# Layer normalisation of a decoder trunk: the last weight panel chunk by chunk with the first sums inside it, one activation table for logarithm and exponential, five mean subtractions on GpSimd, rounded products first

## The reference, cut to what matters

```python
x = layer_norm(DEEPNORM_ALPHA * x + f(x), g, b)

def layer_norm(x, g, b):
    mu = jnp.mean(xf, -1, keepdims=True)
    var = jnp.mean(jnp.square(xf - mu), -1, keepdims=True)
    return (xf - mu) * lax.rsqrt(var + LN_EPS) * g + b
```

## Time and profile before

| what | us |
|---|---|
| median of three runs | 1171.61 |
| the runs | 1167.24 to 1173.54 |
| span of the profiled execution | 1171.3 |
| TensorE busy | 1092.9 (93%) |
| VectorE busy | 704.1 (60%) |
| ScalarE busy | 543.7 (46%) |
| GpSimd busy | 300.1 (26%) |

### The profile page before, as it was taken

One profiled execution on the slowest core, in us unless ns is written; L12 is line 12 of the kernel. 1 busy time (PEld: TensorE's weight loads), 2 busy tenths in 40 slices (PEclk: granted clock), 3 DMA queues, 4 the chain that ended last, 5 costly groups with the idle time before them and its releaser, 6 DMA issues.

```text
span 1171.3 us, 20048 instructions
## 1 busy us (share of the span) xinstructions
PE 1092.9 (93%) x6991; PEld 986.4 (84%) x6991; DVE 704.1 (60%) x1203; ACT 543.7 (46%) x860; POOL 300.1 (26%) x285
## 2 busy tenths in 40 slices
PE   6999979978999998897999999989999799999997
PEld 5999869666666665496999999979999799999996
DVE  4843643677777777548666663365564866665344
ACT  4337511256666666536444443343343544444324
POOL 8400123302677777134000000123003400000111
PEclk9989969988999999898999999989999899999998
DMA  7424200267998996542444443534445244444321
GB/s 228 158 101 149 73 1 1 98 223 259 304 305 307 303 308 219 177 150 72 143 143 143 143 148 130 175 96 143 144 144 153 72 143 147 159 156 157 127 87 46
DMA packets 120882, 182.59 MB, mean 156 GB/s; under 512 B 6224, under 2 KB 61615, under 8 KB 120750
## 3 DMA queue, kind: packets, MB, share of 16 engines
q1 hardware_dynamic: 118402, 174.61, 44.8%
q0 software_dynamic: 2416, 7.16, 2.1%
HBM read 176.12 MB, written 5.63 MB: 155 GB/s over the span
## 4 chain that ended last, share of the span: by engine, by line
PE 80%; DVE 12%; issue 4%; ACT 3%; DMA 1%; POOL 0%; DVEq 0%; SPq 0%; ACTq 0%; POOLq 0%
PE bank L1736 74%; PE bank L2051 4%; DVE kTl L1157 2%; DVE lo L1150 1%; DMA raw<-w_in_mix 1%; ACT hi L751 1%; DVE xres L1583 1%; DVE xres L1157 1%; DVE sbias L1458 1%; PE bank L2253 1%; DVE gs L1454 1%; DVE sbias L1449 1%; PE bank L2184 0%; DVE work L1157 0%; DVE xl L1590 0%
## 5 line engine op out<-in xcount | busy, mean ns | idle before, releaser
L1736 PE MATMUL bank<-xh,hi 128*128 128x320 f32 x1184 | 373.9, 316 | 24.4 <-DVE xl L1590 18.4
L1736 PE MATMUL bank<-xl,hi 128*128 128x320 f32 x1184 | 371.1, 313 | 0.0
L1736 PE MATMUL bank<-xh,lo 128*128 128x320 f32 x1184 | 370.9, 313 | 0.0
L1150 DVE TENSOR_TENSOR lo<-raw,hi 128x2048 fp32r<-128x2048 f32 x102 | 240.4, 2357 | 188.5 <-ACT hi L751 188.5
L751 ACT ACTIVATE hi<-raw 128x2048 fp32r (+2 forms) x124 | 217.9, 1757 | 120.6 <-PE bank L1736 118.3
L1736 PEld LDWEIGHTS bank<-xh,hi 128*128 128x128 f32 x1184 | 227.4, 192 | 28.4 <-issue 25.4
L1736 PEld LDWEIGHTS bank<-xl,hi 128*128 128x128 f32 x1184 | 227.3, 192 | 0.1
L1736 PEld LDWEIGHTS bank<-xh,lo 128*128 128x128 f32 x1184 | 226.9, 192 | 0.0
L1736 PE MATMUL bank<-hh,hi 128*128 128x320 f32 x416 | 129.4, 311 | 1.3 <-DVE hraw L1157 1.3
L1736 PE MATMUL bank<-hh,lo 128*128 128x320 f32 x416 | 128.5, 309 | 0.0
L1736 PE MATMUL bank<-hl,hi 128*128 128x320 f32 x416 | 128.5, 309 | 0.0
(11 more groups left out here) (394 smaller groups left out, 1562.7 us busy)
## 6 DMA issues: line engine op xcount, KB each, us to landing
raw<-w_up SPq DMA_DIRECT2D x44, 1024.0 KB
kring<-cache_k SPq DMA_DIRECT2D x88, 256.0 KB, 3.7
vring<-cache_v SPq DMA_DIRECT2D x84, 256.0 KB, 4.9
raw<-w_down SPq DMA_DIRECT2D x8, 2048.0 KB
raw<-w_in_mix SPq DMA_DIRECT2D x6, 2048.0 KB
raw<-cache_v SPq DMA_DIRECT2D x44, 256.0 KB, 5.0
raw<-cache_k SPq DMA_DIRECT2D x40, 256.0 KB, 3.5
raw<-w_in_sc SPq DMA_DIRECT2D x8, 1024.0 KB
```

Of the source, the lines that this page charges most:

```text
L1150: dve.tensor_tensor(lo[:, p], weight(n)[:, :, 256 * p:256 * p + 256], hi[:, p], ALU.subtract)\
L1736: return pe.matmul(out, lhsT, rhs, start=start, stop=stop, **kw)
```

## The change

It touches what lies around the four layer norms and the order of products in `project`.

- `stats` is cut in two: `first_sums` (GpSimd's two sums, block 6 and its square) and `last_sums` (block 7 and its square). In the last slot of the part, panel 1 is worked through chunk by chunk (all k of chunk 2, then all k of chunk 3), and `first_sums` stands ahead of the last three products of chunk 3; `last_sums` stands after them.
- In every `project` the products go hi·xh, lo·xh, hi·xl instead of hi·xh, hi·xl, lo·xh. In the first chunk of a part the first two wait for `xh` alone, and the wait for `xl` stands ahead of the third.
- ScalarE loads one table set with both functions at the start of `down` and `out_proj`, and no table in `norm`.
- The mean is subtracted on GpSimd for blocks 3 to 7 and on VectorE for blocks 0 to 2. VectorE's order becomes: mean copy, variance (two instructions), blocks 0 and 1, `scaled` 0 and 1, `rest` 0, block 2, and then pairs.
- VectorE's `lo` of the next slot's panel 0 is done in two halves in the last slot of the part, with the residual of block 6 between them.

```diff
@@ gpsimd
                 DV.wait(pool, f"mean{n}")
                 AC.wait(pool, f"sq{n}_7")
-                for m in (KD - 2, KD - 1):
+                PO.wait(pool, f"accq{n}_{KD - 3}")
+                for m in range(3, KD):
                     PO.up(pool.tensor_tensor(xres[:, m, :], xres[:, m, :], lnt[:, 4, :], ALU.subtract), f"centred{n}_{m}")
@@ scalar
             def norm(n, gpack, grow, bpack, brow, following):
-                act.preload_act_table(ACT.Ln)
                 DV.wait(act, f"mean{n}")
@@
             def down(layer, n):
+                act.preload_act_table_set("natural_log_exp_and_others")
@@
             def out_proj(base, n):
+                act.preload_act_table_set("natural_log_exp_and_others")
@@ vector
+            def half_lo(n, k):
+                dve.wait_ge(s["hi_done"], 2 * n + 1)
+                ins = dve.tensor_tensor(lo[:, 0, k:k + 4], weight(n)[:, k:k + 4, 0:256], hi[:, 0, k:k + 4], ALU.subtract)
+                if k:
+                    ins.then_inc(s["lo_done"], 1)
@@ def norm
                 def scaled(m):
-                    if m >= KD - 2:
+                    if m >= 3:
                         PO.wait(dve, f"centred{n}_{m}")
@@
                 DV.wait(dve, f"mean{n}")
-                centre(0)
                 AC.wait(dve, f"msq{n}")
                 PE.wait(dve, f"stat{n}")
                 DV.up(tt(lnt[:, 3, :], bank[5][:, 0:TOK], lnt[:, 2, :], ALU.subtract), f"vara{n}")
                 DV.wait(dve, f"vara{n}")
                 DV.up(dve.tensor_scalar(lnt[:, 3, :], lnt[:, 3, :], 0.0, LN_EPS, ALU.max, ALU.add), f"var{n}")
-                for m in range(1, KD - 2):
-                    ins = centre(m)
-                DV.up(ins, f"centred{n}")
-                DV.wait(dve, f"centred{n}")
+                centre(0)
+                centre(1)
+                DV.wait(dve, f"cent{n}_1")
                 AC.wait(dve, f"rstd{n}")
-                PE.wait(dve, f"stat{n}")
                 scaled(0)
                 scaled(1)
-                for m in range(2, KD):
+                rest(0)
+                centre(2)
+                DV.wait(dve, f"cent{n}_2")
+                for m in range(2, KD, 2):
                     scaled(m)
-                    rest(m - 2)
-                rest(KD - 2)
+                    scaled(m + 1)
+                    rest(m - 1)
+                    rest(m)
                 rest(KD - 1)
@@ out_proj, and down in the same way
                     residual(n, 4 * i + 1, base + i)
-                    split_lo(base + i + 1, 0)
+                    if i < SLOT_OUT - 1:
+                        split_lo(base + i + 1, 0)
+                    else:
+                        half_lo(base + i + 1, 0)
                     residual(n, 4 * i + 2, base + i)
+                    if i == SLOT_OUT - 1:
+                        half_lo(base + i + 1, 4)
                     residual(n, 4 * i + 3, base + i)
@@ tensor, project
                     pe.wait_ge(s["lo_done"], 2 * n + (p + 1))
-                    for k in range(nk):
-                        if p == 0:
+                    order = [(k, j) for k in range(nk) for j in (2 * p, 2 * p + 1)]
+                    if p == 1 and sums:
+                        order.sort(key=lambda kj: kj[1])
+                    for k, j in order:
+                        if p == 0 and j == 0 and rounded:
+                            rounded(k0 + k)
+                        if start and k == 0:
+                            free(j)
+                        if sums and (p, j, k) == (1, 3, nk - 1):
+                            sums()
+                        mm(out, w, xa[:, k0 + k, :], start and k == 0, False)
+                        mm(out, v, xa[:, k0 + k, :], False, False)
+                        if p == 0 and j == 0:
                             ready(k0 + k)
-                        for j in (2 * p, 2 * p + 1):
-                            mm(out, w, xa[:, k0 + k, :], start and k == 0, False)
-                            mm(out, w, xb[:, k0 + k, :], False, False)
-                            ins = mm(out, v, xa[:, k0 + k, :], False, stop and k == nk - 1)
+                        ins = mm(out, w, xb[:, k0 + k, :], False, stop and k == nk - 1)
+                        if ends and k == nk - 1:
+                            ins.then_inc(s["chunk_done"], 1)
@@ feed_forward (the callers of stats, all in this way)
                         project(S_DOWN[layer] + 3 * i + k, hh, hl, nk, free,
-                                lambda q: pe.wait_ge(s["hid_ready"], KF * layer + q + 1), KD * k, k == 0, k == 2)
-                stats(n)
+                                nothing, KD * k, k == 0, k == 2,
+                                rounded=lambda q: pe.wait_ge(s["hid_ready"], KF * layer + q + 1),
+                                sums=(lambda: first_sums(n)) if (i, k) == (1, 2) else None)
+                last_sums(n)
```

More of the change, by code:

```diff
@@ L1634, in down @@
                             residual(n, 4 * i + 1, slot)
-                        if slot + 1 < S_END:
+                        last = (i, k) == (1, 2)
+                        if not last:
                             split_lo(slot + 1, 0)
+                        elif slot + 1 < S_END:
+                            half_lo(slot + 1, 0)
                         if k == 2:
                             residual(n, 4 * i + 2, slot)
+                            if last and slot + 1 < S_END:
+                                half_lo(slot + 1, 4)
                             residual(n, 4 * i + 3, slot)
-                        if (i, k) != (1, 2):
+                        if not last:
                             split_lo(slot + 1, 1)
@@ L1760, in nothing, with project @@
                 pass
-            def project(n, xa, xb, nk, free, ready, k0=0, start=True, stop=True, panels=(0, 1), w0=0, ends=True):
+            def project(n, xa, xb, nk, free, ready, k0=0, start=True, stop=True, panels=(0, 1), w0=0, ends=True, rounded=None,
+                        sums=None):
                 for p in panels:
                     pe.wait_ge(s["lo_done"], 2 * n + (p + 1))
-                    for k in range(nk):
-                        if p == 0:
-                            ready(k0 + k)
-                        for j in (2 * p, 2 * p + 1):
[L1771 to L1775, removed]
-                            mm(out, w, xa[:, k0 + k, :], start and k == 0, False)
-                            mm(out, w, xb[:, k0 + k, :], False, False)
-                            ins = mm(out, v, xa[:, k0 + k, :], False, stop and k == nk - 1)
-                            if ends and k == nk - 1:
-                                ins.then_inc(s["chunk_done"], 1)
@@ L1782, in mix_slot @@
             def mix_slot(i, **kw):
-                project(i, xh, xl, KD, lambda j: pe.wait_ge(s["rel_act"], 4 * i + (j + 1)), lambda k: DV.wait(pe, f"xl{k}"), **kw)
+                project(i, xh, xl, KD, lambda j: pe.wait_ge(s["rel_act"], 4 * i + (j + 1)), lambda k: DV.wait(pe, f"xl{k}"),
+                        rounded=lambda k: AC.wait(pe, f"xh{k}"), **kw)
             DV.wait(pe, "xres5")
@@ L2138, in _, with mean, square, first_sums @@
                         project(S_OUT, xh, xl, 4, nothing, nothing, stop=False, panels=(0,), ends=False)
[L2141 to L2147, removed]
+            def mean(x, start, stop):
+                return mm(bank[4][:, 0:TOK], onesD[:, :], x, start, stop)
+            def square(x, start, stop):
+                return mm(bank[5][:, 0:TOK], onesD[:, :], x, start, stop)
+            def first_sums(n):
                 PO.wait(pe, f"accs{n}_{KD - 3}")
@@ L2196, in free @@
                             pe.wait_ge(s["h_done"], 2 * i + (KF * layer + j - 2 + 1))
-                    project(i + base, xh, xl, KD, free, lambda k: normed_ready(n - 1, k))
+                    project(i + base, xh, xl, KD, free, lambda k: normed_ready(n - 1, k),
+                            rounded=lambda k: AC.wait(pe, f"lnh{n - 1}_{k}"))
                 pe.wait_ge(s["h_done"], KF * (layer + 1) + 2)
@@ L2215, in out_proj @@
                         between()
-                    project(base + i, xa, xb, KD, free0 if i == 0 else lambda j: DV.wait(pe, f"r{n}_{j}"), ready)
-                stats(n)
+                    project(base + i, xa, xb, KD, free0 if i == 0 else lambda j: DV.wait(pe, f"r{n}_{j}"), nothing,
+                            rounded=ready, sums=(lambda: first_sums(n)) if i else None)
+                last_sums(n)
             pe.wait_ge(s["o_lo"], NB)
@@ L2222, in _ @@
             history("f0", KF)
-            project(S_OUT + 1, xh, xl, KD, lambda j: DV.wait(pe, f"r0_{j}"), nothing)
-            stats(0)
+            project(S_OUT + 1, xh, xl, KD, lambda j: DV.wait(pe, f"r0_{j}"), nothing, sums=lambda: first_sums(0))
+            last_sums(0)
             feed_forward(0, 1)
@@ L2232, in free @@
                         pe.wait_ge(s["sc_prod"], 2 * i + (j - 2 + 1))
```

(2 more changed lines are left out.)

26 lines of the change are left out of this document (15 added, 11 removed).

## The result

The changed kernel takes 1175.86 us (median of 15 runs, 1171.57 to 1181.29), the kernel before in the same sessions 1166.43 us. The ratio is 1.0062, with a 95% interval from 1.0042 to 1.0082: about 7.2 us slower (4.9 to 9.6), by over the 0.5% that were set as the bound, though the interval reaches down to 0.42%. Forecast were +4.9 us and, as likeliest (0.63), no difference that can be told; slower by over 0.5% had a chance of 0.32. That 1175.86 lies beside the forecast 1176.2 is partly luck, since the longer series put the kernel before at 1166.43 and not at 1171.6.

What follows compares the result with a forecast made beforehand. TensorE, busy 93% of the span, was taken as the bound, so edits count only where it stands still. Sums +3.3 and what the norms pass on +1.6 made +4.9 us on 1171.3, about 1176.2 us; range for all 1168 to 1180.

Steps and rivals of the forecast that it cites:

- What bounds the kernel, and where to read a norm: TensorE bounds; a norm's worth is read when the mean is copied and when block 5 is scaled.
- The sums inside: Ahead of the mean copy: block 7's residual loses its cover, +0.8 us a norm, +3.3 us in all four.
- The table: In each norm the 1.28 us load goes and the root comes sooner; alone worth nothing, as VectorE's subtractions end later.
- The subtractions: Behind the mean copy: VectorE takes turns with GpSimd's five, about 0.96 us a pair; block 5 scaled +0.6 us later.
- The row of the convolution: Two one-input convolution steps took 1.20 us beside GpSimd's stream, 0.90 without; some 0.15 each, used for the variance's last instruction.
- rival (b): In every norm the variance waits for GpSimd too: +0.4 us each, 1.6 more, 1177.8 us; chance 0.22.
- What norms 0 and 2 pass on: Between `lo` of panel 1 and VectorE's convolution 0.34 us is spare, so of +0.6 some 0.3 and 0.2 are left.
- Rounded first and the small edits: TensorE's earlier restart is hidden, three products stay three in the loops, smaller edits stand in idle time: nothing.
- A sign named for it: TensorE's waits for `xh` and `xl` would be shorter than 18.4 us in sum.
- Norm 3: Without `rest`, two turns behind block 3's scaling delay it and the transposes by +0.5 us.

Runs made afterwards that it cites:

- one table alone: The kernel before with one table set for logarithm and exponential and nothing else changed; ratio 0.9999 to the kernel before.
- the kernel with operands in PSUM: The changed kernel with mean and reciprocal root read by VectorE from PSUM, sums still inside; ratio 0.9982 to the kernel before.

## Why the prediction was right in its mechanism, and too small

**What bounds the kernel, and where to read a norm: right for this change.** The 7.7 us are found at the copy of the mean and behind block 5's scaling. It does not hold for every kernel run here: with one table alone block 5 came 1.1 us sooner and 0.2 to 0.4 arrived, because TensorE then set the pace.

**The sums inside, +0.8 a norm: right.** 0.85 in the trace, and 3.3 us came back when they alone were undone.

**The table, worth nothing by its time: right.** The scalings of the one-table kernel start at the same 4.63 us. That its block 5 came sooner is of another kind (which of GpSimd and VectorE gives way) and not explained.

**The subtractions: the mechanism right, the size too small.** Forecast were GpSimd's five in turns (4.71 us measured from 526.11, 4.7 forecast) and a second input in SBUF as the reason (shown by the kernel with operands in PSUM). The failed step is "by the page it would wait for its end, by the row it loses 0.15, and my sum goes by the row". The variance's last step took 0.82 us instead of 0.37 in all four norms. The GpSimd subtraction that was running when it began, kernel before and then changed kernel:

```profile
529.84 1.17 POOL L682 TENSOR_TENSOR xres<-xres,lnt 128x320 f32<-128x320 f32 x1 [6.77 <-DVE lnt L1594]
```

```profile
526.93 0.86 POOL L683 TENSOR_TENSOR xres<-xres,lnt 128x320 f32<-128x320 f32 x1
```

It ends at 531.01 and 527.79, and the step 0.19 us behind it both times (531.19 and 527.97). So the step waited in both kernels, for the last 0.18 us of GpSimd's first subtraction before, for 0.64 us of its second now. GPSIMD Engine Reference (8. Key points) of the Trainium skill, which names contention with VectorE's two-port modes beside that with two SBUF inputs, was the better guide than the two convolution steps, though no run shows in which mode the variance's step ran. The row of the convolution was no fair sample: its first step began at 546.43, and GpSimd's instruction ended at 546.67, so it had met only 0.24 us of it. With the 0.45 us lost at the variance the chain fell a turn behind, as rival (b) had it: scaling 1 ended 6.09 us after the copy started, where (b) gave 535.3 - 529.27 = 6.03 and the forecast 5.63. This is read from the rows; no kernel frees the variance alone. On top came 0.23 us of VectorE waiting for `xh` of block 0, which was not in the sum. So block 5 came at +1.3 and not +0.6.

**What norms 0 and 2 pass on: wrong.** Forecast was that half is lost in the 0.34 us between `lo` and the convolution. The gap did close (540.73 + 2.94 = 543.67, then 543.71), but the first two convolution steps then took 1.49 us instead of 1.20, beside GpSimd's stream, and gave it all back. The 0.34 us had never been a spare. GpSimd's instruction beside `lo`, kernel before and then changed kernel:

```profile
543.91 2.76 POOL L687 TENSOR_TENSOR xres<-xres,par 128x320 f32<-128x320 f32 x1
```

```profile
541.48 2.76 POOL L688 TENSOR_TENSOR xres<-xres,par 128x320 f32<-128x320 f32 x1
```

It ends 0.58 us behind `lo` in both, and in norm 0 the first convolution step ends 0.20 us behind it in both, though it starts 0.34 us behind `lo` in one and 0.04 in the other. 1.2 us arrived in each norm where 0.3 and 0.2 were forecast. These two norms are 1.9 of the 2.8 us by which the trace (7.7) lies above the forecast (4.9). Some 0.3 each come from this spare; the rest, like norm 1's, comes from the step above, which with about 2 us in three norms is the largest part of the error.

**Rounded first and the small edits, nothing: right.** TensorE's own wait at block 6 grew to 1.30 us, but behind the first two products. A sign named for it did not come: the waits for `xh` and `xl` were to be shorter than 18.4 us in sum and make 17.3 + 3.9 = 21.2.

**Norm 3, +0.5: right** (0.6), in part by luck, since kernels whose VectorE instructions lie the same there ended it up to 0.46 us apart.

Of the cases, rival (b) is what happened, with its own sum again too small (+6.5 forecast, 7.2 measured by the ratio, 7.7 by the trace). It had been given 0.22 against 0.56, on a row of two instructions.

## What to carry to other kernels

Before work is moved to GpSimd beside VectorE, ask which operands both read from SBUF: two-input instructions take turns at about 1 us a pair here, while VectorE with one operand in PSUM runs beside GpSimd undisturbed. Independent work between the last product and the reduction that needs its result covers the latency of the step between them; moved ahead of the product it leaves that latency bare. And where a spare of a few tenths of a microsecond is to swallow a delay, see whether the work behind it would not wait for a neighbour in its new place.

## What the runs showed of the hardware that was not expected

- A VectorE instruction with a single input in SBUF is held up too: the variance's last step took 0.37 us where a GpSimd subtraction had 0.18 us left to run and 0.82 where it had 0.64, and ended 0.19 us behind it each time; reading and writing PSUM, beside the same GpSimd stream, it took 0.50.
- In a meeting of VectorE's two-input stream and one GpSimd instruction, either can give way: GpSimd 0.83 us and VectorE 1.1 us later, or GpSimd 3.60 us and VectorE on time. Both were seen at the same distance from the copy, 7.70 us, in one execution. When GpSimd gives way, its next result is late too, and TensorE waited for it (0.48 us, one table alone).
- After the stop ahead of the last transposes TensorE's granted clock stayed at 0.50 to the end in one kernel and rose to a mean of 0.90 for the second half in another, worth some 0.5 us. It did so between two kernels with the same instructions there, too (13.81 and 14.27 us from the copy to the end).
